# Gated delta rule without precomputed u and w, and other places for the next head's projections

## The reference

```
low = where(strict, einsum(kb, k) * decay, 0)        # kb = k * beta
T = triangular_solve(eye + low, eye)
u = T @ (v * beta)
w = T @ (kb * exp(G))                                # G: cumulated log decay
def step(s, ...):                                    # over the chunks, in order
    v_new = u_c - w_c @ s
    o_c = qd_c @ s + qk_c @ v_new
    s = s * gl_c + kd_c.T @ v_new
```

## Time and profile before

| stretch of the span (us) | what | TensorE busy | VectorE busy | ScalarE busy | GpSimd busy | TensorE clock |
|---|---|---|---|---|---|---|
| 0 to 95.4 | start, gates, first projections | 63.17 | 21.45 | 25.27 | 13.89 | 0.80 |
| 95.4 to 463.7 | 7 turns of the head loop | 346.89 | 242.59 | 130.43 | 144.34 | 1.00 |
| 463.7 to 511.1 | last head | 43.50 | 26.65 | 11.17 | 12.25 | 1.00 |
| 511.1 to 1799.8 | all that follows the heads | 1170.18 | 258.81 | 162.73 | 3.48 | 0.96 |

### The profile page before, as it was taken

How to read it: one execution, slowest core, us unless ns; L and a number is a source line. 1 busy time by engine, 2 the same in 40 slices (tenths; PEclk the granted TensorE clock), 3 DMA queues, 4 the chain that set the end, 5 groups by cost and what they waited for, 6 DMA issues and landing times.

```text
span 1799.8 us, 21591 instructions
## 1 busy us (share of the span) xinstructions
PE 1623.7 (90%) x8392; PEld 1049.0 (58%) x8392; DVE 549.5 (31%) x1122; ACT 329.6 (18%) x664; POOL 174.0 (10%) x180
## 2 busy tenths in 40 slices
PE   5799999999999989979998789998889998999886
PEld 1466666776588868865554369757534543443333
DVE  2266666667520011153122110382500111001002
ACT  2223333433331100021011011341200000000001
POOL 1244343344300000000000000000000000000000
PEclk8799999999999988979999899999899999999998
DMA  9311110111734423419999974103399999999993
GB/s 392 149 54 41 41 47 23 47 35 47 304 139 154 147 87 105 173 50 366 421 421 421 421 287 151 60 1 122 143 417 421 377 368 421 421 362 385 421 421 140
DMA packets 59645, 404.92 MB, mean 225 GB/s; under 512 B 6782, under 2 KB 7938, under 8 KB 13232
## 3 DMA queue, kind: packets, MB, share of 16 engines
q1 hardware_dynamic: 53328, 381.92, 53.3%
q0 software_dynamic: 6240, 21.92, 4.2%
HBM read 402.71 MB, written 1.10 MB: 224 GB/s over the span
## 4 chain that ended last, share of the span: by engine, by line
PE 70%; DMA 17%; DVE 8%; issue 2%; ACT 1%; SPq 1%; DVEq 0%; POOL 0%; POOLq 0%; ACTq 0%
PE bank L602 69%; DMA ring<-in_moe 15%; DVE arena L1631 2%; DMA ring<-in_dense 2%; ACT arena L1264 1%; DVE arena L1662 1%; DVE arena L1678 1%; PE bank L1020 1%; DVE arena L1667 0%; DVE arena L1659 0%; DVE arena L1657 0%; DVE arena L1671 0%; DMA arena<-decay_rows 0%; DVE arena L1681 0%; SPq L434 0%
## 5 line engine op out<-in xcount | busy, mean ns | idle before, releaser
L602 PE MATMUL bank<-ring,arena 128*64 128x512 f32 (+2 forms) x2304 | 519.3, 602 | 60.3 <-DMA ring<-in_moe 58.6
L602 PEld LDWEIGHTS bank<-arena 128*128 128x128 f32 (+2 forms) x2864 | 375.9, 192 | 125.2 <-ACT arena L1264 47.8
L602 PE MATMUL bank<-arena 128*128 128x128 f32 (+3 forms) x2864 | 422.9, 298 | 27.2 <-DVE arena L1681 6.8
L602 PEld LDWEIGHTS bank<-ring,arena 128*64 128x64 f32 (+2 forms) x2304 | 173.8, 137 | 370.2 <-issue 365.0
L1264 ACT ACTIVATE arena<-bank 128x256 f32<-128x256 f32 (+1 forms) x369 | 164.3, 452 | 1175.4 <-PE bank L602 879.2
L602 PE MATMUL bank<-hc,head_w 128*128 128x512 f32 (+1 forms) x384 | 164.8, 536 | 3.1 <-DMA head_w<-in_head_w 3.1
L1997 DVE TENSOR_TENSOR arena<-arena,bank 128x256 f32<-128x256 f32 x48 | 20.2, 421 | 360.2 <-ACT arena L1264 360.2
L602 PE MATMUL bank<-arena,ring 128*128 128x256 f32 x512 | 116.3, 387 | 4.3 <-ACT arena L1264 2.6
L602 PEld LDWEIGHTS bank<-arena,ring 128*128 128x128 f32 x512 | 99.2, 194 | 19.8 <-ACT arena L1264 3.4
L602 PE MATMUL bank<-hc,ring 128*128 128x256 f32 x512 | 110.7, 379 | 0.0
L602 PEld LDWEIGHTS bank<-hc,ring 128*128 128x128 f32 x512 | 97.2, 190 | 13.2
(11 more groups left out here) (245 smaller groups left out, 1054.2 us busy)
## 6 DMA issues: line engine op xcount, KB each, us to landing
ring<-in_moe SPq DMA_DIRECT2D x288, 1024.0 KB, 13.1
ring<-in_dense SPq DMA_DIRECT2D x72, 1024.0 KB, 7.1
head_w<-in_head_w POOLq DMA_DIRECT2D x27, 512.0 KB, 4.0
arena<-decay_rows POOLq DMA_DIRECT2D x16, 256.0 KB, 4.6
xc<-in_xc SPq DMA_DIRECT2D x1, 2048.0 KB, 8.2
arena<-bias_rows POOLq DMA_DIRECT2D x2, 1024.0 KB, 8.7
mats<-in_square SPq DMA_DIRECT2D x1, 1088.0 KB, 11.2
out_y<-xc SPq DMA_DIRECT2D x2, 512.0 KB, 2.9
```

What stands on the lines that cost most here:

```text
L602: return nc.tensor.matmul(out, lhsT, rhs_, start=start, stop=stop, **kw)
```

## The change

`u_`, `w_` and `kb` are gone. The scan instead makes, in every step, `k @ state` (`ks_made`), then on VectorE `vb + (k @ state) * gd["kb"]` in place (`v_left`; `gd["kb"]` now carries a minus sign), then `E @` that on TensorE (`v_made`), and a copy out of PSUM (`v_copied`; ScalarE for step 0, VectorE for the others), which `kd.T @ new_v` reads. By the linearity of `T`, `T @ (v * beta) - T @ (kb * exp(G)) @ s` is `T @ (v * beta - kb * exp(G) @ s)`. The normalised k has a place of its own, `kn`. On VectorE the two scalings by `gd["kb"]` in level 1 are gone, and tap 4 of the convolution of v stands in level 1, behind its two masks. The projections are dealt out as 3, 3, 1, then 9 in the levels, 1 ahead of the inverse's use, and 7 in the scan.

```diff
@@ in build: places in SBUF @@
-        vb, kb, kd = [place(19), place(20)], [place(21), place(22)], [place(23), place(24)]
+        vb, kn, kd = [place(19), place(20)], place(21), [place(23), place(24)]
-        u_, w_ = [place(14), place(15)], [place(16), place(17)]
+        new_v = [place(14), place(15)]
@@ TensorE, head @@
                 ins.then_inc(s["gram"], 1)
-                fill(2)
+                fill(3)
...
                         ins.then_inc(s["y_made"], 1)
-                        fill(1)
+                        if 2 * (k - 1) + g < 9:
+                            fill(1)
...
+                fill(1)
                 pe.wait_ge(s["e_ready"], 4 * h + 4)
-                pe.wait_ge(s["rows_scaled"], 6 * h + 6)
-                for d in range(2):
-                    for a in range(TT):
-                        ins = mm(bank[d][:, a * P:(a + 1) * P], E_[d][:, a, :], vb[d][:, a, :])
-                    ins.then_inc(s["uw_made"], 1)
-                for d in range(2):
-                    for a in range(TT):
-                        ins = mm(bank[2 + d][:, a * P:(a + 1) * P], kb[d][:, a, :], E_[d][:, a, :])
-                    ins.then_inc(s["uw_made"], 1)
+                pe.wait_ge(s["rows_scaled"], 4 * h + 4)
...
                 for n in range(CHUNKS):
-                    for d in range(2):
-                        c = chunk_of(n, d)
-                        if n == 0:
-                            pe.wait_ge(s["uw_copied"], 4 * h + (d + 1))
-                        else:
-                            if n == 1:
-                                pe.wait_ge(s["uw_copied"], 4 * h + (d + 3))
+                    if n > 0:
+                        for d in range(2):
                             pe.wait_ge(s["stepped"], 6 * h + (2 * (n - 1) + d + 1))
-                            mm(bank[d][:, 0:P], w_[d][:, c, :], state[d]).then_inc(s["ws_made"], 1)
+                            mm(bank[d][:, 0:P], kn[:, chunk_of(n, d), :], state[d]).then_inc(s["ks_made"], 1)
                     if n >= QT:
...
-                    fill(1 if n else 0)
+                    if n == 1:
+                        fill(1)
                     for d in range(2):
                         c = chunk_of(n, d)
                         if n > 0:
-                            pe.wait_ge(s["v_new"], 6 * h + (2 * (n - 1) + d + 1))
+                            pe.wait_ge(s["v_left"], 6 * h + (2 * (n - 1) + d + 1))
+                        mm(bank[d][:, 0:P], E_[d][:, c, :], vb[d][:, c, :]).then_inc(s["v_made"], 1)
+                    fill(1)
+                    for d in range(2):
+                        pe.wait_ge(s["v_copied"], 8 * h + (2 * n + d + 1))
                         if n < CHUNKS - 1:
-                            mm(bank[d][:, P:2 * P], kd[d][:, c, :], u_[d][:, c, :]).then_inc(s["kv_made"], 1)
+                            mm(bank[d][:, P:2 * P], kd[d][:, chunk_of(n, d), :], new_v[d][:, chunk_of(n, d), :]
+                               ).then_inc(s["kv_made"], 1)
...
-                    fill(2)
+                    if n < QT:
+                        fill(1)
@@ ScalarE, head @@
-                for i in range(4):
-                    act.wait_ge(s["uw_made"], 4 * h + (i + 1))
-                    dst = (u_ if i < 2 else w_)[i % 2]
-                    act_fn(flat(dst), bank[i][:, :], ACT.Copy).then_inc(s["uw_copied"], 1)
+                for d in range(2):
+                    act.wait_ge(s["v_made"], 8 * h + (d + 1))
+                    act_fn(new_v[d][:, chunk_of(0, d), :], bank[d][:, 0:P], ACT.Copy).then_inc(s["v_copied"], 1)
@@ VectorE, before the heads and head @@
-            link(tt_(gd["kb"][:, :, :], gd["beta"][:, :, :], gd["t"][:, :, :], ALU.mult))
+            link(stt(gd["kb"][:, :, :], gd["beta"][:, :, :], -1.0, gd["t"][:, :, :], ALU.mult, ALU.mult))
...
-                tt_(conv[1], conv[1], norms[1], ALU.mult).then_inc(s["normed"], 1)
+                tt_(kn, conv[1], norms[1], ALU.mult).then_inc(s["normed"], 1)
...
-                conv_taps(h, 2, 2, CONV)
+                conv_taps(h, 2, 2, CONV - 1)
                 for k in range(1, LEVELS):
...
-                    if k < 3:
+                    if k == 1:
+                        conv_taps(h, 2, CONV - 1, CONV)
+                    elif k == 2:
                         dve.wait_ge(s["gram"], 4 * h + 2)
-                        src, dsts = ((gd["kb"], kb), (gd["kd"], kd))[k - 1]
                         for d in range(2):
-                            tt_(dsts[d], bank[7][:, :].rearrange("p (a b) -> p a b", a=TT),
-                                src[:, :, bass.ds(h + HEADS * d, 1)].broadcast_to([P, TT, P]), ALU.mult
+                            tt_(kd[d], bank[7][:, :].rearrange("p (a b) -> p a b", a=TT),
+                                gd["kd"][:, :, bass.ds(h + HEADS * d, 1)].broadcast_to([P, TT, P]), ALU.mult
                                 ).then_inc(s["rows_scaled"], 1)
...
                 for n in range(CHUNKS):
+                    if n == 0:
+                        fill(CONV)
                     for d in range(2):
                         c = chunk_of(n, d)
                         if n > 0:
-                            dve.wait_ge(s["ws_made"], 6 * h + (2 * (n - 1) + d + 1))
-                            dve.wait_ge(s["uw_copied"], 4 * h + 4)
-                            tt_(u_[d][:, c, :], u_[d][:, c, :], bank[d][:, 0:P], ALU.subtract).then_inc(s["v_new"], 1)
-                    fill(1 if n else CONV)
+                            dve.wait_ge(s["ks_made"], 6 * h + (2 * (n - 1) + d + 1))
+                            stt(vb[d][:, c, :], bank[d][:, 0:P], gd["kb"][:, c, bass.ds(h + HEADS * d, 1)], vb[d][:, c, :],
+                                ALU.mult, ALU.add).then_inc(s["v_left"], 1)
+                    for d in range(2):
+                        if n > 0:
+                            dve.wait_ge(s["v_made"], 8 * h + (2 * n + d + 1))
+                            cp(new_v[d][:, chunk_of(n, d), :], bank[d][:, 0:P]).then_inc(s["v_copied"], 1)
...
-                    fill(1)
                 fill(2 * CONV)
```

More of the change, by code:

```diff
@@ L710, in project_head @@
                         else:
-                            pe.wait_ge(s["rows_scaled"], 6 * h)
+                            pe.wait_ge(s["rows_scaled"], 4 * h)
                     moving = hc[:, k, :] if j else H[:, k, :]
@@ L763, in head @@
                 for a in range(TT):
-                    ins = mm(bank[2][:, a * P:(a + 1) * P], conv[1][:, a, :], conv[1][:, a, :])
+                    ins = mm(bank[2][:, a * P:(a + 1) * P], kn[:, a, :], kn[:, a, :])
                 ins.then_inc(s["gram"], 1)
@@ L767, in head @@
                 for a in range(TT):
-                    ins = nc.tensor.transpose(bank[7][:, a * P:(a + 1) * P], conv[1][:, a, :], M("ident"))
+                    ins = nc.tensor.transpose(bank[7][:, a * P:(a + 1) * P], kn[:, a, :], M("ident"))
                 ins.then_inc(s["gram"], 1)
-                fill(2)
+                fill(3)
                 pe.wait_ge(s["first_made"], h + 1)
@@ L780, in head @@
                 for a in range(QT):
-                    ins = mm(bank[6][:, a * P:(a + 1) * P], conv[1][:, QT + a, :], conv[0][:, a, :])
+                    ins = mm(bank[6][:, a * P:(a + 1) * P], kn[:, QT + a, :], conv[0][:, a, :])
                 ins.then_inc(s["gram"], 1)
@@ L849, in head @@
                             c = chunk_of(n, d)
-                            ins = mm(o_part(n, d), u_[d][:, c, :], qk[d][:, c - QT, :], False, n == CHUNKS - 1 and d == 1,
+                            ins = mm(o_part(n, d), new_v[d][:, c, :], qk[d][:, c - QT, :], False, n == CHUNKS - 1 and d == 1,
                                      skip_group_check=True)
```

## The result

The changed kernel takes 1819.78 us (median of 4 runs, 1818.22 to 1824.1) against 1799.19: ratio 1.0112, 95% interval 1.0086 to 1.0137. It is slower, by 16 us more than the forecast of 1803.6 and outside its range.

The account below looks back on a forecast made before the run. TensorE was taken as nearly full, a head being its issue time plus waits. Terms 1.16 - 0.25 - 0.54 + 0.23 = +0.60 per head, x 7 = +4.2, took 1799.36 to 1803.6 us; range 1794 to 1809.5.

Parts of the forecast that it names:

- Part 1: Level 1 to 2: tap 4 behind the masks delays ScalarE's activation and copy, so TensorE's x starts later; +1.16 us per head.
- the upper bound of 1.74: Tap 4's move, with GpSimd's mask at its old time: x of level 2 starts at 267.70, +1.74 us per head.
- idle for about 1.7 us: Sign that the forecast is right: TensorE idles about 1.7 us ahead of x of level 2, in its first half.
- Part 2: Projections elsewhere: free ahead of level 0 and the inverse's use, a gain in the last levels; -0.25 us per head.
- Part 3: The scan, from the last mask's end to the next head's first matmul: shorter by 0.54 us per head.
- rival 2: Scan hand-overs lie bare, about 0.95 per step for three steps; half bare gives +1.4 per head, 1813; chance 0.06.
- Part 4: Next head's start: GpSimd's line 546 holds VectorE's first line, the first Gram matmul comes later; +0.23 us per head.
- The last head: The last head, treated apart from the seven turns: taken as 0, between -1 and +1.
- Rival 1: GpSimd's mask stays where it was: +1.74 in place of +1.16, +1.18 per head, 1807.7, slower; chance 0.14.
- rival 3: TensorE's issue time decides alone, the activation doesn't hold the copy: -1.22 per head, 1790.8, faster; chance 0.12.
- rival 4: Level 2's delay is soaked up in levels 4 to 6: head at 0.0, 1799.4, no change; chance 0.13.
- a head over 53.6: Sign that the forecast is wrong: a scan hop is bare, seen as TensorE idle behind `v_left` or a copy.

Follow-up runs that it names:

- Experiment 5: The changed kernel with GpSimd's two decays of q (line 567) moved behind its mask of level 4: 1818.0 us, 1.0083 of the kernel before.
- experiment 6: The changed kernel with ten extra matmuls that nobody reads in TensorE's wait ahead of x of level 2: 1814.84 us, 1.0072 of the kernel before.
- experiment 8: The changed kernel with activation of v behind ScalarE's first copy of level 2, decays of q behind level 4's mask, line 546 ahead of the last load: 1798.25 us, 0.9957.
- experiment 3: The changed kernel with tap 4 back ahead of the masks and the projections dealt out as before: 1798.97 us, 0.9976 of the kernel before.
- experiment 2: The changed kernel with tap 4 back ahead of the masks of level 1: 1809.16 us, 1.004 of the kernel before.
- experiment 4: The changed kernel with tap 4 back ahead of the masks and GpSimd's load issue (line 505) behind its mask of level 4: 1814.04 us, 1.0056.
- experiment 7: The kernel before with only tap 4 moved behind the masks of level 1: 1840.52 us, 1.0194 of the kernel before.

## Why the prediction was wrong

The path was right, one size on it and one thing beside it were not.

- **Part 1, the failed step: "So tap 4 ends at 265.57 + 0.55 = 266.12".** Everything up to it held: tap 4 starts 11.77 after the mark as forecast, line 505 follows line 527 at once, the mask runs 11.00 after the mark (forecast 11.01), the activation and then the copy wait for the tap, and TensorE for them. But the tap's price was one outcome, taken from the last head, where the tap was let in right behind the mask. Line 567 was queued behind the mask both there and here, and the prediction never looked at it; here its first product goes ahead of the tap. The term was +1.16 and measured +1.83; the upper bound of 1.74 was for another cause. Experiment 5 moved line 567 away and tap 4 took 1.07. Why the tap wins in the last head and loses in the turns is not shown. Over seven heads: 4.7 us of the miss.
- **The clock was in no term.** I wrote 1.00 for the loop and never asked what a wait of two us would do to it, though the longest wait in the loop had been 1.0. 4.2 us by the three turns' lengths; experiment 6 shows it and gives back 4.0 (its first turn still has 54.42, so 0.3 of the first turn's 1.57 is not the clock). The wait itself I had forecast ("idle for about 1.7 us"), and experiment 5 shows falls behind 1.83 already.
- **Part 2** -0.25, measured -0.26; the places in front of level 0 and of the inverse cost nothing, as said.
- **Part 3** -0.54, measured -0.40: 1.0 us over seven heads. Up to step 2 the starts of TensorE's rows are within 0.03 of the forecast. The two stretches without a projection in steps 2 and 3 take 1.54 (194.84 to 196.38) and 2.53 (197.24 to 199.77), forecast 1.48 and 2.36, and the 0.10 for the loop's end did not come. So the hops there are bare by 0.22 and 0.33 in all, not by half of 0.95 in each of three steps; rival 2 falls.
- **Part 4** +0.23, measured +0.34 and 0.11 for a restart: 1.5 us. The mechanism was the one named (1.79 for line 1646, forecast 1.7 to 1.9): line 546 starts 0.92 after the head's start, forecast 0.83, and the restart of 0.11 was in no term; experiment 8 moves line 546 out of the way and gets 3.87 for 4.27.
- **The last head** 0, measured -0.3.
- Rival 1 falls by the rows of GpSimd, rival 3 by the copy behind the activation, rival 4 by the quiet turn, which keeps all of the delay. Forecast per quiet head +0.60, measured +1.61. One of the prediction's own signs misleads here: a head over 53.6 was to mean a bare hop of the scan, and the heads of 54.15 come from tap 4.

What remains of the 15.0 once these are added is 0.5 the other way: before, the first and last turn were 0.2 to 0.3 longer than the middle ones.

The change as a whole, in heads of the profiles: the formula without u and w -0.67 (experiment 3), the new places +1.27 with tap 4 where it was (experiment 2), tap 4's move +1.0 more and the clock +0.6.

## What to carry to other kernels

Before an operation that feeds the next engine is moved behind another, look at the in-order queue it feeds, and at everything GpSimd has queued at that time, not only at the instruction that overlaps it now: give the operation a range from "behind the first" to "behind all of them", since both were seen. A pause in an engine that is off the critical path may be what keeps an operation on the path short; find out whose wait makes that pause before changing what it waits for. And when a change puts one wait of two us in front of a full TensorE, ask for the granted clock behind it.

## What was not expected of the hardware

- A VectorE operation with two operands in SBUF that meets GpSimd can lose not one but up to three of its instructions: tap 4 took 0.75 alone, 1.07 and 1.09 behind a mask, 1.75 behind a mask and one 128x256 product, 2.87 behind a mask and two. Each time it ended 0.55 or 0.56 after the last of them. It does not always lose: with a mask and two products queued it went in behind the mask in the last head before (1.83) and in experiment 4 (2.23), behind one product in the changed kernel. The Trainium skill ("SBUF — State Buffer", section "SBUF: two separate sides") has a port pair that the two engines share locked for the whole instruction and the other side fully blocked; the trace agrees on the block. Why GpSimd's next instruction is let in ahead of one that already waits, and why once in one place and three times in another, is open.
- Tap 4 also stretched from 0.75 to 1.59 beside GpSimd's issue of a weight load (experiment 2), though none such shows in the kernel before, where its first 0.37 lay beside the issues of line 527 and the rest in a pause. Whether the issue itself holds the port was not tried apart.
- TensorE's granted clock fell to 0.50 after a wait of 1.83 us in six of seven heads (experiment 5), of 1.86 in three of seven (experiment 4), of 2.50 in three of seven (the changed kernel), of 3.62 in all seven (experiment 7), and in none where ten matmuls filled it or where the wait was 1.21 (six heads of experiment 2). It cost about 1.3 us each time, in experiment 7 about 2.4. Why a wait of 2.50 was followed by a fall less often than one of 1.83 is open.
